# Moving the low halves of the column weights to VectorE, making one mask first, and using other banks for the last turn

## The reference

```
h = RMSNorm(x);  proj = h @ w_in -> q, k, v, index q/k/w, glu, gate_a, gate_c
A: indexer scores -> top 256 keys per query (a mask) -> attention -> w_attn_out
B: u = a * sigmoid(b) from glu -> causal depthwise conv, 31 taps -> LayerNorm -> swish -> w_conv_out
x += (sigmoid(gate_a) * A + sigmoid(gate_c) * B) @ w_out
x += (silu(h2 @ w_gate) * (h2 @ w_up)) @ w_down,   h2 = RMSNorm(x)
```

## Time and profile before

| what | us |
|---|---|
| median of three runs | 1997.84 |
| the profiled execution's own time | 1996.86 |
| its span, first to last instruction | 1995.1 |
| PE busy | 1872.1 (94%) |
| DVE busy | 1094.6 (55%) |
| ACT busy | 766.1 (38%) |
| POOL busy | 261.0 (13%) |
| mean granted TensorE clock | 0.979 |

### The profile page before, as it was taken

How to read it: one execution, slowest core, us unless ns; L and a number is a source line. 1 busy time by engine, 2 the same in 40 slices (tenths; PEclk the granted TensorE clock), 3 DMA queues, 4 the chain that set the end, 5 groups by cost and what they waited for, 6 DMA issues and landing times.

```text
span 1995.1 us, 28433 instructions
## 1 busy us (share of the span) xinstructions
PE 1872.1 (94%) x11088; PEld 1647.4 (83%) x11088; DVE 1094.6 (55%) x1712; ACT 766.1 (38%) x1471; POOL 261.0 (13%) x287
## 2 busy tenths in 40 slices
PE   6977999999989966988999999999999999999998
PEld 3533799899989944656988889999999999999997
DVE  1045799897988977776454343333443333433333
ACT  2235655622367147765122233333223333333321
POOL 1001122122296022330000000000000000000000
PEclk9988999999999988999999999999999999999999
DMA  7110110332121323775321133333433333433332
GB/s 210 17 54 18 46 43 27 107 102 91 62 66 44 99 89 109 267 249 215 137 111 43 32 147 126 127 125 124 162 114 122 121 122 123 157 125 126 126 126 105
DMA packets 74236, 220.28 MB, mean 110 GB/s; under 512 B 14197, under 2 KB 25109, under 8 KB 65315
## 3 DMA queue, kind: packets, MB, share of 16 engines
q1 hardware_dynamic: 67963, 205.05, 30.3%
q10 hardware_dynamic: 6192, 14.16, 1.8%
HBM read 197.26 MB, written 21.89 MB: 110 GB/s over the span
## 4 chain that ended last, share of the span: by engine, by line
PE 56%; ACT 2%; DVE 1%; issue 1%; DVEq 0%; ACTq 0%
PE ps L653 17%; PE ps L652 17%; PE ps L651 17%; PE ps L881 1%; PE ps L858 1%; ACT buf L1260 1%; PE ps L915 1%; PE ps L900 1%; PE ps L871 1%; DVE buf L1571 1%; PE ps L971 0%; PE ps L887 0%; DVE buf L1396 0%; ACT buf L1250 0%; ACT buf L1302 0%
## 5 line engine op out<-in xcount | busy, mean ns | idle before, releaser
L651 PE MATMUL ps<-buf,buf 128*128 128x384 f32 (+2 forms) x2364 | 830.7, 351 | 17.3 <-DVE buf L1396 11.7
L653 PE MATMUL ps<-buf,buf 128*128 128x384 f32 (+2 forms) x2364 | 832.6, 352 | 0.0
L652 PE MATMUL ps<-buf,buf 128*128 128x384 f32 (+2 forms) x2364 | 830.7, 351 | 0.0
L651 PEld LDWEIGHTS ps<-buf,buf 128*128 128x128 f32 x2364 | 446.6, 189 | 43.2 <-DVE buf L1396 10.0
L652 PEld LDWEIGHTS ps<-buf,buf 128*128 128x128 f32 x2364 | 446.5, 189 | 24.3
L653 PEld LDWEIGHTS ps<-buf,buf 128*128 128x128 f32 x2364 | 446.2, 189 | 24.3
L1396 DVE TENSOR_TENSOR buf<-buf,buf 128x1024 fp32r<-128x1024 f32 (+4 forms) x245 | 335.6, 1376 | 184.2 <-ACT buf L1374 39.1
L1744 DVE TENSOR_TENSOR buf<-buf,ps 128x384 f32<-128x384 f32 x66 | 36.5, 553 | 403.1 <-PE ps L653 403.1
L1519 DVE SCALAR_TENSOR_TENSOR buf<-buf,buf,buf 128x1024 f32<-128x1024 f32 x240 | 197.4, 864 | 4.0
L1372 ACT ACTIVATE buf<-ps 128x384 f32<-128x384 f32 x66 | 32.5, 492 | 295.9 <-PE ps L653 295.9
L1374 ACT ACTIVATE buf<-buf 128x384 fp32r<-128x384 f32 x66 | 34.7, 525 | 282.1 <-DVE buf L1744 282.1
(11 more groups left out here) (182 smaller groups left out, 1746.5 us busy)
## 6 DMA issues: line engine op xcount, KB each, us to landing
buf<-in_w_ffn SPq DMA_DIRECT2D x67, 1024.0 KB, 5.6
buf<-in_w_ffn SPq DMA_DIRECT2D x66, 512.0 KB, 3.6
buf<-in_cache_k SPq DMA_DIRECT2D x16, 1024.0 KB, 7.3
buf<-in_cache_v SPq DMA_DIRECT2D x16, 1024.0 KB, 10.5
buf<-in_w_cols SPq DMA_DIRECT2D x24, 512.0 KB, 4.1
buf<-in_x SPq DMA_DIRECT2D x18, 512.0 KB, 3.7
gate_scr<-buf ACTq DMA_DIRECT2D x16, 576.0 KB, 4.8
buf<-gate_scr SPq DMA_DIRECT2D x16, 576.0 KB, 5.2
```

Source lines behind the costliest of these rows:

```text
L651: mm(dst, whi, xhi, start=start, stop=False)
L652: mm(dst, whi, xlo, start=False, stop=False)
L653: return mm(dst, wlo, xhi, start=False, stop=stop)
```

## The change

VectorE makes the low halves of the column weights instead of GpSimd: three ahead of the search, one after each of the search steps 3, 5, 8, 10, 13, 15, 18, 20, 23, 25, 28 and 30, two behind the search, four between masks, three between taps, 24 in all. The number of taps ahead of `qkv_low(0)` stays 20. The mask `scoreS` is made first, and SP writes it out with the load of column 20 instead of 22, waiting for one mask instead of seven. GpSimd keeps the products u. For the last of the nine turns of h2, banks 0 and 1 take the place of 6 and 7: it waits for the x1 of tile 6 (the last user of those banks) instead of `f_made`, and the waits for its evacuation move behind the second `gate_up`. A further `wo_done` is raised after k = 1 of the second half of `out_tile(8)`: `gu_low(1, 0)` waits for it, the x1 of tile 8 and SP for the end of the tile as before.

```diff
 # SyncE
-                if t == NCOL - 2:
-                    sp.wait_ge(S("mask_made"), NSEL)
+                if t == NCOL - 4:
+                    sp.wait_ge(S("mask_made"), 1)
                     sp.dma_start(A["mask_scr"], scoreS).then_inc(S("mask_out"), 16)
...
-            sp.wait_ge(S("wo_done"), NT)
+            sp.wait_ge(S("wo_done"), NT + 1)
 # TensorE, turn_h2, out_tile, group(0)
+        def h2_bank(t):
+            return 0 if t == NT - 1 else 6
-                if t:
+                if t == NT - 1:
+                    pe.wait_ge(S("x1_made"), (NT - 2) * 2)
+                elif t:
                     pe.wait_ge(S("h2T_split"), t * 2)
...
+                        if t == NT - 1 and f == 1 and k == 1:
+                            l.then_inc(S("wo_done"), 1)
...
                     gate_up(g, 0, 0)
-                    pe.wait_ge(S("f_made"), 1)
                     turn_h2(NT - 1)
-                    pe.wait_ge(S("h2T_split"), 2 * NT)
-                    pe.wait_ge(S("x1_made"), 2 * NT)
                 else:
                     gate_up(g, 0, 0)
                 gate_up(g, 1, 1)
+                if isinstance(g, int):
+                    pe.wait_ge(S("h2T_split"), 2 * NT)
+                    pe.wait_ge(S("x1_made"), 2 * NT)
                 down(g, 0, 0, first=True)
 # VectorE
+            def col_low(t):
+                dve.wait_ge(S("col_high"), t + 1)
+                low(wcollo[:, t % 4], wcol[:, t % 4], wcolhi[:, t % 4]).then_inc(S("col_split"), 1)
+            for m in range(3):
+                col_low(m)
...
+            col_steps = [3 * t - 3 * t // 6 for t in range(1, 13)]
             for bit in range(31, -1, -1):
...
+                if 31 - bit in col_steps:
+                    col_low(3 + col_steps.index(31 - bit))
+            for t in (15, 16):
+                col_low(t)
             count(ALU.is_gt, tiles)
...
-            for n, (sc, L) in enumerate(select):
+            for i, n in enumerate([NSEL - 1] + list(range(NSEL - 1))):
+                sc, L = select[n]
+                if i in (0, 2, 3, 5):
+                    col_low(17 + (0, 2, 3, 5).index(i))
...
-            convolve(20)
+            for t in range(21, NCOL):
+                col_low(t)
+                convolve(4)
+            convolve(8)
             qkv_low(0)
...
                 if t == NT - 1:
                     gu_low(1, 0)
+                    dve.wait_ge(S("wo_done"), NT + 1)
 # GpSimd
-            for m in range(3):
-                col_low(m)
...
-            for t in range(NCOL - 3):
-                col_low(t + 3)
-                if t < NGLU and t % 2:
+            for t in range(NGLU):
+                if t % 2:
```

More of the change, by code:

```diff
@@ L967, in turn_h2 @@
                 pe.wait_ge(S("h2_made"), t + 1)
-                if t:
+                if t == NT - 1:
+                    pe.wait_ge(S("x1_made"), (NT - 2) * 2)
+                elif t:
                     pe.wait_ge(S("h2T_split"), t * 2)
                 for k in range(KD):
-                    l = nc.tensor.transpose(bank(6, w=2)[:, tok(k)], xs[:, t % 2, k * P:(k + 1) * P], ident)
+                    l = nc.tensor.transpose(bank(h2_bank(t), w=2)[:, tok(k)], xs[:, t % 2, k * P:(k + 1) * P], ident)
                 l.then_inc(S("h2_turned"), 1)
@@ L1345, in turned_h2 @@
                 for f in range(2):
-                    ac(h2hi[:, 4 * f:4 * f + 4, tok(t)], bank(6 + f).rearrange("p (k t) -> p k t", k=4), ACT.Copy)\
+                    ac(h2hi[:, 4 * f:4 * f + 4, tok(t)], bank(h2_bank(t) + f).rearrange("p (k t) -> p k t", k=4), ACT.Copy)\
                         .then_inc(S("h2T_made"), 1)
@@ L1496, in _ @@
             ch.link(ve.tensor_scalar(rest, cnt, -1.0, float(TOPK), ALU.mult, ALU.add))
-            for n, (sc, L) in enumerate(select):
-                if n:
-                    dve.wait_ge(S("mask_made"), n)
+            for i, n in enumerate([NSEL - 1] + list(range(NSEL - 1))):
+                sc, L = select[n]
+                if i in (0, 2, 3, 5):
+                    col_low(17 + (0, 2, 3, 5).index(i))
+                if i:
+                    dve.wait_ge(S("mask_made"), i)
                 ch.link(ve.tensor_scalar(hit[:, 0:L], sc, thrf[:, n:n + 1], None, ALU.is_equal))
@@ L1713, in h2_low @@
                 for f in range(2):
-                    low(h2lo[:, 4 * f:4 * f + 4, tok(t)], bank(6 + f).rearrange("p (k t) -> p k t", k=4),
+                    low(h2lo[:, 4 * f:4 * f + 4, tok(t)], bank(h2_bank(t) + f).rearrange("p (k t) -> p k t", k=4),
                         h2hi[:, 4 * f:4 * f + 4, tok(t)]).then_inc(S("h2T_split"), 1)
@@ L1872, in _ @@
                         else:
-                            pool.wait_ge(S("mask_made"), b - 1)
+                            pool.wait_ge(S("mask_made"), b)
                             gp.tensor_tensor(nb[n % 2], score[b][:, (b - 1) * P:(b + 1) * P], near[:, h], ALU.add)\
```

## The result

The changed kernel has a median of 1984.6 us over six runs (1983.4 to 1988.8), beside 1997.8 for the kernel before: a ratio of 0.9934 with a 95% interval of 0.9921 to 0.9948, or 13.2 us. Forecast were 1986.0 and 11.5 us, in a range of 1981 to 1996: the time, its range and the sign held. The two large terms held less exactly than the sum, as the traces show.

What follows compares the result with a forecast made beforehand. PE, busy 94% of the span, was taken as the bound, leaving its idle time and lower-clock stretches to win. Column stage -3.5 and tail -8.0 gave -11.5 us: 1986 us against the median, range 1981 to 1996.

Steps and rivals of the forecast that it cites:

- The two large terms: Column stage 3.5 us earlier (bounds -1 and 6) and tail 8.0 us earlier (bounds 3 and 8.5).
- What bounds the column stage: Column stage: PE stalls on late ACT, which waits for VectorE's search, held up 19 us beside GpSimd's col_low.
- The 6.1 us of stalls and clock: Column stage: PE stalls of 2.1 and 2.3 us plus 1.7 us of lower clock, which a change could return.
- The stall at column 13: Column stage: low ready at 385.6, PE wants it at 384.2; 2.5 us taken, bounds 0 and 5.
- The end of the taps moves with PE: Between columns and attention: VectorE's 11.7 us of waits for q/k/v copies take up its earlier gains or losses.
- Masks: Behind the search: the 10.4 us wait for mask_out goes, against up to some 13 us waiting for high halves.
- The tail: From out_tile(8) to the second gate_up's product: gaps and lower clock go, 8.4 us worked out, 8.0 taken.
- the clock's term: Tail: clock at 0.53 over 6 us, nearly all at 1.2 GHz, costs 2.8 us that would be saved.
- The three waits: Tail: PE's waits of 2.48 us for gu_low(1, 0), 0.65 for f_made and 2.50 for the last h2 turn go.
- A: Rival, column stage: products u hold up VectorE the whole 2.9 us each; net -3, about 1994 us; chance 0.17.
- B: Rival, search: VectorE becomes the bound, long rows not caused by GpSimd's col_low; about +11, 2008 us; chance 0.06.
- C: Rival, tail: a later FFN load delays the second gate_up; tail wins 3 instead of 8, about 1991; chance 0.15.

Runs made afterwards that it cites:

- pool_memset: Kernel before, with GpSimd writing zeros by memset where it made the column weights' low halves, which are left out; 1990.2 us (one run).
- mask_last: Changed kernel with the masks in their old order and SP's old wait for all seven at column 22; 1984.5 us, ratio 0.9934.
- cols_only: Changed kernel with both edits of the tail undone, so lows on VectorE and mask first remain; 1993.8 us, ratio 0.9980.
- banks_only: Kernel before with only the other banks for the last h2 turn, its waits moved; no earlier gu_low(1, 0); 1991.8 us, ratio 0.9975.
- early_only: Kernel before with only the further wo_done, so gu_low(1, 0) runs inside out_tile(8); the last turn keeps its banks; 1994.6 us, ratio 0.9983.

## Why the prediction was right, and where not

- **What bounds the column stage: right.** GpSimd's lows held up VectorE's short operations, that made ACT late, and that stalled PE. `pool_memset` shows the cause by itself. The 6.1 us of stalls and clock that the stage was said to hold came back whole: 6.47; the 0.4 above it was not followed.
- **The stall at column 13: wrong, and the term mis-sized.** Step 25 began 133.6 us after step 0, not 136.05. A low costs 1.14 us in the search, not 1.25 (a step with a low behind it takes 5.94 instead of 4.80), and the four products hold up VectorE by 1.6, 0.6, 0.6 and 0.6 us, 3.4, where 4.8 were taken. So the low of column 13 (382.07 + 1.22) ended at 383.3 instead of 385.6. PE wanted it at 384.2 by the prediction's count, 0.75 later in this execution. No stall, and the 2.5 us set aside for one were not spent; 3.5 became 6.5, just past the upper bound of 6.
- **"The end of the taps moves with PE": half right.** It does move with PE's q/k/v stage: from ACT's fourth copy to attention it is 75.99 us before and 76.00 after. VectorE came to `qkv_low(1)` 0.7 us earlier than before, counted from the columns' start (bounds of 3 earlier and 5 later), so the waits did hold. The failed step was to take that stage as fixed, and VectorE's waits in it as free. PE came 6.5 us earlier and VectorE only 0.7, the wait at `qkv_low(1)` was used up, and through GpSimd PE lost 1.9 us. So of the 6.5 us, 4.6 reached attention: 1.1 more than the 3.5 forecast, from one term too small and one left out.
- **Masks: right on the wait, and nothing won.** No wait for the mask is left, as said, and waiting beside PE's columns took its place, 17.3 us against "up to some 13". `mask_last` shows that the order changes nothing. SP issued the mask's write at 435.66 without a hold-up; the prediction had the load due near 437.
- **The tail: right, with some luck in the clock's term.** 8.44 us where 8.4 were worked out and 8.0 taken. The three waits go but for 0.16 us, and no lower clock is left. That the sum meets 8.4 so closely is partly luck: the 2.8 us were read from one execution, and tails left as before lose 1.7 (`cols_only`) and 3.4 (`pool_memset`) in theirs. `banks_only` and `early_only` show that one gap left is enough for a lower clock. It came close: PE waits 0.16 us for `gu_low(2, 1)`, where the prediction put that low 0.1 us ahead of PE.
- **The rivals.** A asked for 2.9 us at each product: it was 1.6 at most. That is due to where the products fall, which the prediction only estimated: in `pool_memset` three of them hold a short operation up to 2.33 us. B asked for a cause of the 2.2 us rows other than GpSimd: `pool_memset` excludes that. The page that spoke for B by its first half ("Perfetto Trace Analysis" of the Trainium skill, section "Optimizing Scalar/DVE Operations") was borne out by its second half, that moving work between VectorE and GpSimd may not help: moving it back helped. C asked for a late FFN load: ACT's copy behind that load starts 5.1 us after SP's first issue behind `out_tile(8)`, before (1146.52 to 1151.61) and after (1142.13 to 1147.23), so the load did not land later.
- **The sum.** By the trace -6.5 + 1.9 - 8.4 = -13.0 against the -11.5 of the forecast; the rest up to the measured 13.2 is less than the spread of the unchanged stages.

## What to carry to other kernels

Work of GpSimd that nobody waits for is not free where VectorE runs short operations: price it by the hold-up of whoever meets it, and give it to VectorE when it is shorter there (1.14 us of search for a low, against 2.2 of hold-up). When an engine's waits are called slack, ask who runs better while it waits, and look for work behind the wait that could be moved into it: of the waits left after this change, filling them with taps gave another 10 us. Judge the gaps of one place together: one that stays can keep the lower clock behind it, and what that clock costs in one execution is not what it costs in the next.

## What the runs showed of the hardware

- The hold-up goes both ways. A GpSimd operation on 128x256 takes 0.74 us beside an idle VectorE, 1.33 beside its taps and 2.33 beside a 2.29 us low; a VectorE operation on 7 elements takes 0.17 us alone and 2.33 beside a GpSimd product of 2.40.
- A memset on GpSimd, which reads nothing, still holds up VectorE's operations with one tensor input: 0.97 instead of 0.17 us beside a memset of 0.95.
- Each of the five kernels that kept a gap of PE of 2.5 us in the tail had a stretch at a lower granted clock behind one (0.53 to 0.84 in the windows read); in the five where at most 0.27 us were left it stayed at 1.00. The first gap, of 2.5 us, was followed by 1.00 in the kernel before and in `cols_only`, and by 0.72 over 6 us in `pool_memset`: what decides there stays open.
